# Modulation rows on GpSimd and ScalarE, and a layer norm whose squares are summed on VectorE

## The reference

```python
mod = jax.nn.silu(c) @ w_ada[l] + b_ada[l]          # c: 1 x 1024, w_ada: 1024 x 6144
sh1, sc1, g1, sh2, sc2, g2 = jnp.split(mod[:, None, :], N_MOD, axis=-1)
h = rms_norm(x, norm_mix_g[l]) * (1.0 + sc1) + sh1
proj = jnp.einsum('bsd,de->bse', h, w_in[l])
b_s, c_s, v_s, v_c, gl_c, gate_br = jnp.split(proj, SPLITS[:-1], axis=-1)
y_a = b_s * causal_dwconv(c_s * v_s, conv_short_w[l])            # 3 taps
y_a = jnp.einsum('bsc,cd->bsd', y_a, w_short_out[l])
u = v_c * jax.nn.sigmoid(gl_c)
u = causal_dwconv(u, conv_conf_w[l]) + conv_conf_b[l]            # 31 taps
u = jax.nn.silu(layer_norm(u, conf_ln_g[l], conf_ln_b[l]))
y_b = jnp.einsum('bsc,cd->bsd', u, w_conf_out[l])
g_a, g_b = jnp.split(jax.nn.sigmoid(gate_br), 2, axis=-1)
mix = jnp.einsum('bsd,de->bse', g_a * y_a + g_b * y_b, w_o[l])
x = x + g1 * mix
```

## Time and profile before

| | |
|---|---|
| median of 3 runs | 2115.03 us (2111.46 to 2122.49) |
| profiled execution | 2113.76 us, of which the profiled span is 2111.8 us |
| granted TensorE clock, mean | 0.991 |
| TensorE matmul busy | 2040.6 us (97%), 9452 instructions |
| VectorE | 1115.6 us (53%), 1422 |
| ScalarE | 816.2 us (39%), 1096 |
| GpSimd | 745.9 us (35%), 549 |
| read from HBM | 211.31 MB, 101 GB/s over the span |

### The profile page before, as it was taken

How to read it: one execution, slowest core, us unless ns; L and a number is a source line. 1 busy time by engine, 2 the same in 40 slices (tenths; PEclk the granted TensorE clock), 3 DMA queues, 4 the chain that set the end, 5 groups by cost and what they waited for, 6 DMA issues and landing times.

```text
span 2111.8 us, 29388 instructions
## 1 busy us (share of the span) xinstructions
PE 2040.6 (97%) x9452; PEld 1651.8 (78%) x9452; DVE 1115.6 (53%) x1422; ACT 816.2 (39%) x1096; POOL 745.9 (35%) x549
## 2 busy tenths in 40 slices
PE   7999999999998999999999999999998989999997
PEld 6777788888886776788888877888887777888886
DVE  6666444454465666454453455799955542332323
ACT  6455454222253444444222255422226345322224
POOL 1111277872133333277861144444442021101012
PEclk9999999999999999999999999999999999999999
DMA  4222244543333333334543332323332222333332
GB/s 150 70 63 66 80 140 136 182 139 100 98 111 80 81 88 80 100 129 142 178 138 99 99 110 70 99 90 98 91 98 82 88 80 90 99 93 95 100 98 101
DMA packets 62733, 218.20 MB, mean 103 GB/s; under 512 B 7648, under 2 KB 7776, under 8 KB 62560
## 3 DMA queue, kind: packets, MB, share of 16 engines
q1 hardware_dynamic: 59616, 213.43, 31.6%
q0 software_dynamic: 3072, 4.20, 1.5%
HBM read 211.31 MB, written 2.10 MB: 101 GB/s over the span
## 4 chain that ended last, share of the span: by engine, by line
PE 85%; DVE 4%; POOL 4%; issue 4%; ACT 3%; DMA 1%; SPq 0%; POOLq 0%; DVEq 0%; ACTq 0%
PE G L1292 27%; PE G L1293 26%; PE G L1294 26%; PE Z L1401 1%; PE O L1419 1%; PE Z L1382 1%; POOL qkv L1159 1%; ACT wh L339 1%; DVE wl L645 1%; DVE stay L733 1%; DVE sp L750 0%; DMA qkv<-tmp 0%; POOL kl L1149 0%; DMA raw<-stream 0%; POOL ql L1149 0%
## 5 line engine op out<-in xcount | busy, mean ns | idle before, releaser
L339 ACT ACTIVATE wh<-raw 128x1024 fp32r<-128x1024 f32 x348 | 368.8, 1060 | 971.1 <-PE G L1294 905.2
L1292 PE MATMUL G<-xh,wh 128*128 128x512 f32 x1640 | 651.8, 397 | 24.8 <-DVE xl L650 8.7
L1293 PE MATMUL G<-xl,wh 128*128 128x512 f32 x1640 | 641.8, 391 | 0.0
L1294 PE MATMUL G<-xh,wl 128*128 128x512 f32 x1640 | 641.3, 391 | 0.0
L645 DVE TENSOR_TENSOR wl<-raw,wh 128x1024 fp32r<-128x1024 f32 x292 | 440.6, 1509 | 241.2 <-ACT wh L339 237.6
L1292 PE MATMUL G<-yh,wh 128*128 128x512 f32 x960 | 379.4, 395 | 16.5 <-DVE wl L645 10.5
L1292 PEld LDWEIGHTS G<-xh,wh 128*128 128x128 f32 x1640 | 309.8, 189 | 101.3 <-issue 25.1
L1293 PE MATMUL G<-yl,wh 128*128 128x512 f32 x960 | 375.6, 391 | 0.0
L1294 PE MATMUL G<-yh,wl 128*128 128x512 f32 x960 | 375.0, 391 | 0.0
L1294 PEld LDWEIGHTS G<-xh,wl 128*128 128x128 f32 x1640 | 309.7, 189 | 65.7
L1293 PEld LDWEIGHTS G<-xl,wh 128*128 128x128 f32 x1640 | 310.0, 189 | 62.4 <-issue 1.0
(11 more groups left out here) (188 smaller groups left out, 1793.8 us busy)
## 6 DMA issues: line engine op xcount, KB each, us to landing
raw<-stream SPq DMA_DIRECT2D x348, 512.0 KB, 3.5
araw<-ada_w SPq DMA_DIRECT2D x48, 512.0 KB, 4.2
qkv<-tmp POOLq DMA_DIRECT2D x64, 64.0 KB, 4.0
h<-x_t SPq DMA_DIRECT2D x8, 256.0 KB, 6.3
out_t<-h SPq DMA_DIRECT2D x8, 256.0 KB, 2.4
con<-const_d SPq DMA_DIRECT2D x1, 1344.0 KB, 9.8
vec<-vec_d SPq DMA_DIRECT2D x1, 212.0 KB, 3.7
```

Source lines behind the costliest of these rows:

```text
L339: eng.activation(wh[s][:, :, :], raw[s][:, :, :], ACT.Copy).then_inc(w_hi, 1)
L1292: eng.matmul(total[:, :], wh[s][:, k, :], src_h[:, k, :], start=k == 0, stop=False)
L1293: eng.matmul(total[:, :], wh[s][:, k, :], src_l[:, k, :], start=False, stop=False)
L1294: mm = eng.matmul(total[:, :], wl[s][:, k, :], src_h[:, k, :], start=False, stop=k == kt - 1)
```

## The change

The modulation weights are handed over transposed, so that a tile holds 128 whole columns of `w_ada` as rows of 1024 numbers, and c is handed over repeated on all 128 partitions (a new input `c_row`, 512 KB). GpSimd multiplies a tile by silu(c) in place; ScalarE copies it in place with an accumulator output that gives the column of mod. There are four buffers; loops that went two by two go four by four. TensorE has no part in it, and bank M goes. In the layer norm, VectorE adds the squares itself, through PSUM bank Z[0], between the centrings; gate b tiles are copied raw from PSUM (`keep_b`) and get their sigmoid later in place (`gate_b`); `output` moves behind the layer norm; the statistic, the spread and the splits take other places, and U_CO runs unit by unit.

```diff
+ROWS = 4
-        cs = sb("cs", [P, KD])
+        cs = sb("cs", [P, D])
+        adac = sb("adac", [P, 2 * ADA_TILES])
-            araw = [sb(f"araw{s}", [P, KD, P], F32, r) for s in range(2)]
+            araw = [sb(f"araw{s}", [P, D], F32, r) for s in range(ROWS)]
...
@@ sync
             def load_ada(j, s):
-                wait(eng, ada_sum, j - 1)
+                wait(eng, ada_sum, j - ROWS + 1)
...
+                if which == 0:
+                    eng.dma_start(cs[:, :], c_row).then_inc(in_c, 16)
                 def beside_up(w):
-                    for s in range(2):
-                        load(2 * w + u + s, 0)
-                        load(2 * w + u + s, 1)
-                        load_ada(2 * w + j + s, s)
+                    for s in range(ROWS):
+                        load(ROWS * w + u + s, 0)
+                        load(ROWS * w + u + s, 1)
+                        load_ada(ROWS * w + j + s, s)
...
@@ scalar
-                            eng.activation(cs[:, :], vec[:, V_C:V_C + KD], ACT.Silu).then_inc(cs_ready, 1)
...
+            def sum_ada(j, s):
+                eng.wait_ge(ada_times, j + 1)
+                eng.activation(araw[s][:, :], araw[s][:, :], ACT.Copy, accum_out=col(adac, j)).then_inc(ada_sum, 1)
...
+                    if which < 2 and part < 2:
+                        with eng.Fori(0, nt // ROWS) as w:
+                            for s in range(ROWS):
+                                unit(ROWS * w + s)
+                                sum_ada(ROWS * w + j + s, s)
...
+                        with eng.Fori(0, KD // ROWS) as w:
+                            for s in range(ROWS):
+                                split_hi(ROWS // 2 * w + u + s // 2 + 1, s % 2)
+                                if which < 2 and part == 0:
+                                    sum_ada(ROWS * w + j + s, s)
...
             residual(U_WO[0], Q_FFN0, V_FFN0)
+            eng.wait_ge(in_c, 16)
+            eng.activation(cs[:, :], cs[:, :], ACT.Silu).then_inc(cs_ready, 1)
...
+            def keep_b(n):
+                u, s = U_GB + n // 2, n % 2
+                split_b(n)
+                eng.wait_ge(used, 2 * u + s + 1)
+                eng.activation(sgb[:, n, :], G[s][:, :], ACT.Copy).then_inc(evac[s], 1)
             def gate_b(n):
-                u, s = U_GB + n // 2, n % 2
-                eng.wait_ge(used, 2 * u + s + 1)
-                eng.activation(sgb[:, n, :], G[s][:, :], ACT.Sigmoid).then_inc(evac[s], 1)
+                eng.wait_ge(evac[n % 2], U_GB + n // 2 + 1)
+                eng.activation(sgb[:, n, :], sgb[:, n, :], ACT.Sigmoid).then_inc(gated, 1)
...
-            for n in range(4):
-                if n < 2:
-                    for m in range(4 * n, 4 * n + 4):
-                        square(m, m % 2, 8 * Q_VAR + m, acc, centred, m + 1)
-                split_b(n)
-                gate_b(n)
+            for m in range(6):
+                deviation(m)
+            keep_b(0)
+            for m in range(6, KD):
+                deviation(m)
+            keep_b(1)
+            keep_b(2)
             for n in range(KD):
                 ln_hi(n)
-                if n % 4 == 2:
-                    split_b(4 + n // 4 * 2)
-                if n % 4 == 3:
-                    gate_b(4 + n // 4 * 2)
-                    split_b(5 + n // 4 * 2)
-                    gate_b(5 + n // 4 * 2)
+                if n in (2, 5, 7):
+                    keep_b({2: 3, 5: 4, 7: 5}[n])
+            for n in range(6):
+                gate_b(n)
+            for n in (6, 7):
+                keep_b(n)
+            for n in (6, 7):
+                gate_b(n)
@@ vector
                     taps(t, m, 4)
-                    output(n)
...
+            def add_deviation(n):
+                eng.wait_ge(sq_ready, KD * Q_VAR + n + 1)
+                if n == 1:
+                    eng.tensor_tensor(Z[0][:, :], sq[0][:, :], sq[1][:, :], ALU.add).then_inc(sq_added, 2)
+                else:
+                    eng.wait_ge(sq_added, KD * Q_VAR + n)
+                    eng.tensor_tensor((Z[0] if n < KD - 1 else ssum)[:, :], Z[0][:, :], sq[n % 2][:, :],
+                                      ALU.add).then_inc(sq_added, 1)
...
-            for n in range(KD):
-                eng.tensor_tensor(acc[:, n, :], acc[:, n, :], tmp[0][:, :], ALU.subtract).then_inc(centred, 1)
-                if n in (3, 7):
-                    split_lo(U_GB + 1, n // 4)
-            statistic(S_VAR, LN_EPS, between=(U_GB + 2, 0))
+            for n in range(3):
+                centre(n)
+            gate_a(KD - 1)
+            for n in range(3, KD):
+                centre(n)
+                if n < KD - 1:
+                    add_deviation(n - 2)
+            for n in range(KD - 3, KD):
+                add_deviation(n)
+            statistic(S_VAR, LN_EPS)
...
+            eng.wait_ge(w_lo, 2 * (U_GB + 3))
+            split_lo(U_GB + 3, 0)
+            for n in range(KD // 2):
+                output(n)
+            split_lo(U_GB + 3, 1)
+            for n in range(KD // 2, KD):
+                output(n)
+            split_lo(U_CO, 0)
             split_lo(U_CO, 1)
@@ gpsimd
-            def fold_ada(j, s):
...
+            def times_ada(j, s):
+                eng.wait_ge(ada_land[s], 16 // ROWS * (j + ROWS - s))
+                eng.tensor_tensor(araw[s][:, :], araw[s][:, :], cs[:, :], ALU.mult).then_inc(ada_times, 1)
...
-            eng.wait_ge(var_ready, S_MEAN + 1)
-            clear(5)
-            add_round(Q_VAR)
-            inverse_root(S_VAR, 6)
+            split_lo(U_GB + 1, 0)
+            inverse_root(S_VAR, 5)
+            split_lo(U_GB + 1, 1)
+            for s in range(2):
+                split_lo(U_GB + 2, s)
@@ tensor
-                        project(10, 17)
-                        eng.wait_ge(modc_ready, 1)
-                        project(17, 24)
+                        project(10, 24)
...
-            def modulation(j, s):
-                eng.wait_ge(ada_sum, j + 1)
-                eng.matmul(col(M, j), asum[s][:, :], ones[:, 0:1], start=True, stop=True).then_inc(ada_mm, 1)
...
-            product(u, 1, yh, yl, s_lo, 0, ks=range(0, 4))
+            product(u, 1, yh, yl, s_lo, 0, ks=range(0, 2))
             eng.wait_ge(tap_d, NV_OPS * KD)
             eng.matmul(O[:, :], ones, ssum[:, :], start=True, stop=True).then_inc(stat, 1)
-            product(u, 1, yh, yl, s_lo, 0, ks=range(4, KD))
-            steps(U_GB, 1, xh, xl, mod_lo, 0)
+            product(u, 1, yh, yl, s_lo, 0, ks=range(2, KD))
+            product(U_GB, 0, xh, xl, mod_lo, 0)
+            product(U_GB, 1, xh, xl, mod_lo, 0, ks=range(0, 5))
+            statistic(sq_added, KD * (Q_VAR + 1))
+            product(U_GB, 1, xh, xl, mod_lo, 0, ks=range(5, KD))
             u = U_GB + 1
-            product(u, 0, xh, xl, mod_lo, 0)
-            product(u, 1, xh, xl, mod_lo, 0, ks=range(0, 2))
-            statistic(sq_added, KD * (Q_VAR + 1))
-            product(u, 1, xh, xl, mod_lo, 0, ks=range(2, KD))
+            product(u, 0, xh, xl, mod_lo, 0, ks=range(0, 2))
             spread_root(S_VAR)
+            product(u, 0, xh, xl, mod_lo, 0, ks=range(2, KD))
+            product(u, 1, xh, xl, mod_lo, 0)
             steps(u + 1, 2, xh, xl, mod_lo, 0)
-            both(U_CO, yh, yl, u_lo, 0)
-            steps(U_CO + 1, 3, yh, yl, u_lo, 0)
+            steps(U_CO, 4, yh, yl, u_lo, 0)
```

More of the change, by code:

```diff
@@ L489, in ffn, with unit @@
                 for part, nt in enumerate(PARTS):
-                    with eng.Fori(u, u + nt) as v:
-                        n = v - u
+                    def unit(n):
+                        v = n + u
                         split_hi(v + 1, 0)
@@ L506, in ffn @@
                             eng.activation(tile(hid, n), csb[:, :], ACT.Copy).then_inc(a_hi, 1)
[L507 to L511 removed]
+                    j = ADA_TILES * which + (PARTS[0] + KD) * part
+                    if which < 2 and part < 2:
[4 more added lines that the diff above has]
+                    else:
+                        with eng.Fori(0, nt) as n:
+                            unit(n)
+                    u, f, j = u + nt, f + nt, j + nt
+                    if part < len(PARTS) - 1:
+                        with eng.Fori(0, KD // ROWS) as w:
+                            for s in range(ROWS):
+                                split_hi(ROWS // 2 * w + u + s // 2 + 1, s % 2)
+                                if which < 2 and part == 0:
+                                    sum_ada(ROWS * w + j + s, s)
                     else:
@@ L930, in _ @@
             eng.tensor_tensor(gfe[:, :], vec[:, V_FIN:V_FIN + KD], vec[:, V_FIN:V_FIN + KD], ALU.mult).then_inc(gfe_sum, 1)
-            eng.wait_ge(ada_mm, half)
-            eng.tensor_tensor(modc[:, 0:half], M[:, 0:half], vec[:, V_ADA:V_ADA + half], ALU.add).then_inc(modc_ready, 1)
+            eng.wait_ge(ada_sum, half)
```

(27 more changed lines are left out.)

94 lines of the change are left out of this document (37 added, 57 removed).

## The result

The changed kernel takes 2094.85 us (median of 4 runs, 2093.41 to 2096.09), against 2116.72 us of the kernel before in 4 runs beside it: ratio 0.9902, interval 0.9884 to 0.9919. Predicted were 2095.3. By the medians side by side it is 21.9 us.

A forecast was written before the change was run, and what follows sets the result against it. TensorE's own work was taken as the bound (busy 2040.6 of 2111.8 us). Savings 10.3 + 1.6 + 1.1 + 6.7 = 19.7 us off 2113.76 gave 2094.1, with 1.3 for the median 2095.3; range 2087 to 2106 us, 8 in 10.

The forecast's parts named there:

- Columns: Modulation matmuls leave TensorE in the feed-forward stages: 44 of 48 columns count, at 0.235 us each, 10.3 us saved.
- The four columns taken as hidden: Last two columns of each layer: removing them saves nothing, as TensorE then waits longer for the last hidden tile.
- The fold's waits: First down projection of both layers: four buffers end TensorE's wait for a late weight tile, 2 x 0.8 = 1.6 us.
- Rival D: Fold's waits: the stall at 370 is the DMA's and the sums eat the rest; 2097 to 2105 us, chance 0.07.
- ScalarE's sums at nothing: 48 new ScalarE sums of 1.25 us, 60 us in all, cost TensorE 0, with bounds 0 and 2 us.
- rival C: ScalarE's ordered queue: sums delay the splits, down-projection steps take 7.35 us in place of 5.44; 2126 us, chance 0.05.
- GpSimd's multiplication: Modulation fold on GpSimd: one multiplication per tile, 1.9 us, in place of five and a half.
- The head: First attention slot: both halves come about 1.4 us earlier and TensorE's wait of 1.1 us goes, 1.1 us saved.
- Layer norm: U_GB to U_CO: four low-half waits go, waits of 1.6 (statistic) and 2.7 us (U_GB+3) come; 6.7 us saved.
- rival A: The layer norm stage only exchanges its waits; 13.0 us saved in all, 2102.0 us, chance 0.15.
- The outputs: Outputs h*WF leave the conv stage, where TensorE never waits for VectorE: nothing gained, 0.
- The likeliest case: The forecast itself, all terms together: 19.7 us off, 2095.3 us, chance 0.62.

The follow-up runs named there:

- the two-buffer kernel: The changed kernel with two row-tile buffers in place of four (ROWS = 2): 2120.36 us, ratio 1.0032.
- the added copies: The changed kernel with one more, unused ScalarE copy of 128x3072 ahead of each of the 48 sums: 2093.19 us, ratio 0.9898.
- The other bank: The changed kernel with the first value product in bank O in place of Z[3]: 2092.11 us, ratio 0.9886.
- rows: The kernel before with only the modulation part of the change, layer norm stage and gate tiles as before: 2096.39 us, ratio 0.9929.
- first square into PSUM: The changed kernel with ScalarE writing the square of tile 0 straight into PSUM bank Z[0]: 2092.66 us, ratio 0.9892.
- all three: The changed kernel with first value product in bank O, U_GB+3's first low half made earlier, and first square written to PSUM: 2087.31 us, ratio 0.9872.
- early squares: "all three" with the first two squares ahead of ScalarE's split of U_GB's second tile, additions one tile behind the centrings: 2088.28 us, ratio 0.9875.
- rows and steps: "rows" plus one line of the layer norm part, U_CO run product by product: 2098.83 us, ratio 0.9913.

## Why the prediction was right, and where it was not

**Columns: right, a little small.** In the second part, eight units went from 89.12 to 87.04 us, 0.26 us a column, where I had 0.235. The four columns taken as hidden are: after them TensorE's wait for the last hidden tile grew from 0.57 to 1.04 us. 44 columns gave 12.9 - 1.6 = 11.3 us, 0.257 each, against 10.3.

**The fold's waits: right.** 1.6 us, and the two-buffer kernel shows the cause. Rival D falls.

**ScalarE's sums at nothing: right**, and rival C falls, by the added copies. That the loads beside the high halves would vanish was right too. GpSimd's multiplication was not: 2.41 us in the median, 2.52 on average, and not 1.9. The product that I took the price from has one full operand and a small repeated one; this one has two full tiles. It costs nothing, since the tile is issued a unit ahead.

**The head: wrong.** The wait of 1.1 us was to go. ScalarE's load and GpSimd's low half did come earlier, and the wait stayed at 1.09 us with another name, `qkv`. GpSimd had k ready at 29.7 us, but the masks also wait until VectorE has emptied the bank of the first value tile, at 30.9, and VectorE had waited for TensorE:

```profile
27.60 2.13 POOL L1198 TENSOR_TENSOR kl<-qkv,kh 128x512 fp32r<-128x512 f32 x1
```

```profile
30.21 0.69 DVE L755 TENSOR_TENSOR qkv<-Z,rstd 128x512 f32<-128x512 f32 x1 [1.63 <-PE Z L1335]
```

The other bank removed the wait. The trace before already had both conditions, and VectorE's ended 0.2 us ahead of GpSimd's (30.68 and 30.88 us, TensorE at 31.04), so 0.2 us was the most that an earlier k could give:

```profile
28.76 2.12 POOL L1149 TENSOR_TENSOR kl<-qkv,kh 128x512 fp32r<-128x512 f32 x1
```

```profile
29.99 0.69 DVE L724 TENSOR_TENSOR qkv<-Z,rstd 128x512 f32<-128x512 f32 x1 [0.24 <-PE Z L1294]
```

The step that failed: "both halves come about 1.4 us earlier [...] and the wait of 1.1 us is gone". I looked at who released the wait and not at what else it holds for. That the first product came 1.0 us earlier is no part of the change: in the kernels here that share the changed kernel's start it comes anywhere from 7.4 to 9.0 us (7.65 after, 8.66 before).

**Layer norm: right in sum and places, wrong in cause.** 5.0 us against 6.7. The waits are where I put them: 2.2 (1.6 predicted) at the statistic, 2.2 (2.7) at U_GB+3, none at U_CO. The lower clock followed the first, and not the second (0.94 and 1.00 in the rows above), so the clock's price fell on the other wait than I had it. But over the U_GB units the stage is 52.2 us, as before: here the squares on VectorE, the raw gates and the moved statistic exchanged waits, and what rival A said is true of them. The gain is U_CO unit by unit, which one line brings. I had added up waits gone and waits come over the whole stage; per edit the sum is about zero for the many and 3.5 for the one, and the rest of the 5.0 is the clock. With 5.0 in the stage A's time (2102.0) falls, its mechanism does not.

The size comes apart like this. At full clock I had the stretch end at 1641.4, 60.5 us behind the start of U_GB; the two-buffer kernel, at full clock, took 61.5, so 1.0 us of work was missing from my chain. I had the additions all read PSUM, but the first one has both operands in SBUF and took 1.91 us. The lower clock then cost its full 1.6 us, where I had taken half. And part of the 6.7 was never the edits' to give: the kernel before had 6.8 us of this stretch at the lower clock, and "rows", the same code without them, took 2.9 us less.

**The outputs: wrong.** They were "0", with the reason that TensorE never waits for VectorE in the conv stage. It does, for a bank that VectorE empties late, and the move is worth 2.3 us (in the conv stage's part of the result above). The list of waits does not name VectorE there; it has them under "issue", 3.9 us in 5 waits before and 1.7 in 2 after, a line that the prediction did not take up. VectorE, busy for 97% of the time from 1400 to 1520 us before, was the sign.

**The total** agrees within 0.5 us because errors offset: columns +1.0, head -1.1, layer norm -1.7, outputs +2.3, the earlier first product +1.0, and -2.1 us from stretches at the lower clock and pauses that fell elsewhere. The likeliest case was right; half a microsecond of agreement is luck.

## What to carry to other kernels

A releaser in the list of waits is the last condition of several: before a wait is booked as gone, list all that the instruction waits for, with the time of each. Where a change has many edits in one stage, work out what each gives by itself, as one of them may carry it all; in the layer norm stage a product order did. An engine that is almost always busy should not be put down as "nobody waits for it" from the list of waits alone: compare the starts of the waiting engine's products, too. A load that waits for a free buffer holds every load behind it in its queue, so two more buffers for the least important stream were worth 25 us.

## What the runs showed of the hardware

**Two operands in SBUF beside GpSimd.** The average of 1.36 us for a centring beside GpSimd hides what happens. In the traces here a VectorE instruction with both operands in SBUF that starts more than 0.2 us into one of GpSimd's ends 0.55 to 0.56 us behind GpSimd's end, whenever it began. That is so in all eight such centrings and additions of the changed kernel, "first square into PSUM", "all three" and "early squares"; they are 1.12 to 1.91 us long, against 0.68 otherwise. Additions that read PSUM took 0.69 to 0.70 us in the middle of GpSimd's splits. It looks as if the one waited for the other to end, and not as if both ran slower. So what counts is how much of GpSimd's instruction is left, up to 2.4 us.

**The clock.** The same wait is not always followed by the lower clock. In the first attention slot TensorE waits 2.8 us at 212 us in both kernels. The granted clock from 208 to 216 us is 0.79 before and 1.00 after:

```profile
208.00:216.00 8.00, 5.19 (x23) 4.26 (x21) 6.65 (x10) 2.38 (x5) 0.00 (x0) 0.79 0.01 5
```

```profile
208.00:216.00 8.00, 5.18 (x35) 4.00 (x33) 6.59 (x9) 2.92 (x6) 0.00 (x0) 1.00 0.00 0
```

In those 8 us the same engine did 23 matmuls in one and 35 in the other. Two executions of other kernels here, "rows" and "rows and steps", differ there in the same way (1.00 and 0.81). Such stretches add up to about the same in both executions (31 us at the lower level before, 31 after, without the tail), but they move between stages, as the conv stage's 6.8 and 13.6 us show. That is why a stage of one profile tells an edit of 1 us apart only where its waits are looked at too. What decides it stays open.
